# Score matmuls of an even and an odd head issued together, over two score banks, in one attention of a three-network kernel

## What is computed

```
scores = q[h] @ k[group].T / 8          # 256 x 512 for each head
o[h]   = softmax(scores) @ v[group]
cv     = depthwise_conv31(glu)          # 512 channels
y      = silu(layer_norm(cv) * g + b)
h      = h + gate * (concat(o, y) @ w_out)
```

## Time and profile before

| what | value |
|---|---|
| median of 3 runs | 2510.86 us |
| runs | 2505.34, 2510.86, 2511.07 us |
| profiled execution, its own time | 2511.8 us |
| its span in the profile | 2509.7 us |
| TensorE matmul busy | 2049.2 us (82% of the span) |
| VectorE busy | 586.2 us (23%) |
| ScalarE busy | 322.7 us (13%) |
| GpSimd busy | 122.8 us (5%) |
| mean DMA rate | 253 GB/s over the span |

### The profile page before, as it was taken

One profiled execution on the slowest core, in us unless ns is written; L12 is line 12 of the kernel. 1 busy time (PEld: TensorE's weight loads), 2 busy tenths in 40 slices (PEclk: granted clock), 3 DMA queues, 4 the chain that ended last, 5 costly groups with the idle time before them and its releaser, 6 DMA issues.

```text
span 2509.7 us, 30195 instructions
## 1 busy us (share of the span) xinstructions
PE 2049.2 (82%) x12607; PEld 1211.2 (48%) x12607; DVE 586.2 (23%) x1650; ACT 322.7 (13%) x784; POOL 122.8 (5%) x164
## 2 busy tenths in 40 slices
PE   7999999897555666798765656669899999979999
PEld 3444547564222222485322322234578744547874
DVE  1223335822000000223000000033524302332330
ACT  1023311221000000102000000011411101201110
POOL 0100003600000000000000000011000000000000
PEclk9999999589888778899978787879899999969999
DMA  9876763017999999953999999984044335303430
GB/s 356 325 262 228 277 209 137 31 59 305 425 426 426 426 427 426 323 191 120 424 425 427 426 426 425 426 308 154 31 134 157 145 105 181 101 18 125 160 118 17
DMA packets 190494, 634.46 MB, mean 253 GB/s; under 512 B 7393, under 2 KB 89457, under 8 KB 157640
## 3 DMA queue, kind: packets, MB, share of 16 engines
q1 hardware_dynamic: 186000, 623.84, 64.1%
q0 software_dynamic: 1472, 5.76, 0.6%
q10 hardware_dynamic: 2936, 3.66, 0.4%
HBM read 632.14 MB, written 1.09 MB: 252 GB/s over the span
## 4 chain that ended last, share of the span: by engine, by line
PE 62%; DMA 30%; DVE 5%; ACT 1%; issue 1%; POOL 1%; SPq 0%; POOLq 0%; DVEq 0%; ACTq 0%
DMA ring<-in_moe_w_down 30%; PE bank L573 18%; PE bank L588 16%; PE bank L2126 6%; PE bank L1788 4%; PE bank L669 2%; PE bank L901 2%; PE bank L632 2%; PE bank L859 2%; PE bank L660 2%; PE bank L497 1%; PE bank L1772 1%; PE bank L1805 1%; DVE arena L1339 1%; PE bank L1149 1%
## 5 line engine op out<-in xcount | busy, mean ns | idle before, releaser
L1772 PE MATMUL bank<-ring,arena 128*32 128x256 f32 x4096 | 316.3, 465 | 198.9 <-DMA ring<-in_moe_w_up 122.0
L588 PE MATMUL bank<-hT,ring 128*128 128x256 f32 x1920 | 423.2, 384 | 4.3 <-DVE arena L2167 3.0
L588 PEld LDWEIGHTS bank<-hT,ring 128*128 128x128 f32 x1920 | 369.8, 193 | 57.5 <-issue 6.1
L573 PE MATMUL bank<-ring,hT 128*128 128x512 f32 (+3 forms) x864 | 356.1, 571 | 7.9 <-DVE hT L523 3.5
L1772 PEld LDWEIGHTS bank<-ring,arena 128*32 128x32 f32 x4096 | 143.7, 128 | 357.5 <-DMA ring<-in_moe_w_up 158.8
L573 PEld LDWEIGHTS bank<-ring,hT 128*128 128x128 f32 x864 | 161.6, 192 | 191.7 <-issue 188.7
L1788 PE MATMUL bank<-ring,arena 128*32 128x256 f32 x2048 | 168.7, 488 | 83.0 <-DMA ring<-in_moe_w_down 73.7
L1788 PEld LDWEIGHTS bank<-ring,arena 128*32 128x32 f32 x2048 | 76.4, 134 | 162.2 <-DMA ring<-in_moe_w_down 80.6
L2126 PE MATMUL bank<-ring,arena 128*128 128x512 f32 x352 | 151.4, 592 | 0.0
L1628 DVE TENSOR_TENSOR arena<-arena,bank 128x256 f32<-128x256 f32 x32 | 13.5, 421 | 513.2 <-ACT arena L1688 513.2
L2126 PEld LDWEIGHTS bank<-ring,arena 128*128 128x128 f32 x352 | 66.9, 190 | 83.3 <-issue 83.2
(11 more groups left out here) (319 smaller groups left out, 1682.6 us busy)
## 6 DMA issues: line engine op xcount, KB each, us to landing
ring<-in_moe_w_gate SPq DMA_DIRECT2D x64, 2048.0 KB, 26.7
ring<-in_moe_w_up SPq DMA_DIRECT2D x64, 2048.0 KB, 26.1
ring<-in_moe_w_down SPq DMA_DIRECT2D x64, 2048.0 KB, 26.1
ring<-in_ada_w SPq DMA_DIRECT2D x24, 2048.0 KB, 13.0
ring<-in_w_up SPq DMA_DIRECT2D x44, 1024.0 KB, 7.5
ring<-in_w_in SPq DMA_DIRECT2D x11, 2048.0 KB, 13.3
ring<-in_w_down SPq DMA_DIRECT2D x10, 2048.0 KB, 7.9
ring<-in_w_out SPq DMA_DIRECT2D x6, 2048.0 KB, 7.9
```

What stands on the lines that cost most here:

```text
L573: ins = t_.matmul(bank[b][:, 0:n], lhsT(k)[:, P * t:P * t + P], w[:, k, c0:c0 + n], start=(k == 0), stop=(k == kt - 1))
L588: ins = t_.matmul(bank[b][:, 256 * (j % 2):256 * (j % 2) + 256], w[:, k, P * j:P * j + P], rhs[:, k, :], start=(k == 0), stop=(k == 7), sk ...
L1772: ins = t_.matmul(bank[4][32 * j:32 * j + 32, at:at + 256], xs_now[b][:, 4 * (c % 2) + k, :], w[:, k, 256 * j:256 * j + 256], start=(c % 2 ...
```

## The change

The even layer's attention goes through the same branch as the others: at an even step the scores of units i and i+1 are issued back to back, at an odd step none. `units2` is reordered so that the units of a pair are the two heads 2·h2 and 2·h2 + 1 with the same half of the queries. The score banks of this attention become TWO (4 and 2) on all three engines, so that the scores of unit i wait for the exponential of unit i-2. Nothing else is changed; the steps of the work beside the attention keep their numbers.

```diff
@@ attention_pe
             ahead = len(scores)
-            paired = tag != "b2"
...
             for i in range(len(units) + 3):
-                if i < len(units) and not paired:
-                    score_bank_free(i)
-                    score(i)
-                elif i < len(units) and i % 2 == 0:
+                if i < len(units) and i % 2 == 0:
                     score_bank_free(i)
                     score_bank_free(i + 1)
                     score(i)
                     score(i + 1)
@@ units2
-        for h in range(8):
-            g, lo = h // 4, HD * (h % 2)
-            for t in range(2):
-                units2.append(unit(pair(qxT, h, t), kxT[lo:lo + HD, g, :], [kv[:, k, P + HD * g:P + HD * g + HD] for k in range(4)],
-                                   512, qx[:, t, HD * h:HD * h + HD]))
+        for h2, t, m in itertools.product(range(4), range(2), range(2)):
+            h = 2 * h2 + m
+            g, lo = h // 4, HD * m
+            units2.append(unit(pair(qxT, h, t), kxT[lo:lo + HD, g, :], [kv[:, k, P + HD * g:P + HD * g + HD] for k in range(4)],
+                               512, qx[:, t, HD * h:HD * h + HD]))
@@ even_pe, even_act, even_dve
-            attention_pe("b2", units2, before=turned("kx", kx_items) + turned("qx", qx_items), also=layer_norm_sums)
+            attention_pe("b2", units2, before=turned("kx", kx_items) + turned("qx", qx_items), also=layer_norm_sums, scores=TWO)
-            attention_act("b2", units2, before=[(dve_s, "glu1")], also=squares)
+            attention_act("b2", units2, before=[(dve_s, "glu1")], also=squares, scores=TWO)
-            attention_dve("b2", units2, also=conv_and_norm)
+            attention_dve("b2", units2, also=conv_and_norm, scores=TWO)
```

## The result

The changed kernel takes 2516.2 us in the median of 14 runs, against 2511.59 us for the kernel before in its own 14. The ratio is 1.002, with a 95% interval of 1.0011 to 1.0029: 4.6 us slower by the medians, a difference that many runs resolve, though it lies inside the 0.3% that the prediction called no change. The forecast was 2517.3 us, from a working that gave +6.4.

A forecast was written before the change was run, and what follows sets the result against it. TensorE and VectorE were taken as tied in the even layer's attention. VectorE's stalls +5.3, steps 12 to 15 0 and clock +1.0 gave +6.3, say 6.4 us: median 2517.3 us, range 2507 to 2524.

The forecast's parts named there:

- What bounds the kernel: Even layer's attention: TensorE ends the chain, VectorE has no slack; at most some 1.5 us of TensorE's saving can count.
- The cost of a pair: Two 512-key score products of neighbouring heads overlap and cost what one does: 2.00 us low clock, 1.05 full.
- The wait and what is queued behind it: Even steps 4 to 10: late pairs delay P times V, stalling VectorE's output and the taps queued behind: +5.3 us.
- Steps 12 to 15 and the clock: End of the even layer's attention: later small sums offset by a saved score, 0; earlier clock fall, +1.0 us.
- After the stage: Behind the even layer's attention: nothing absorbs a shift; expert weights and the weight traffic move with the attention's end.
- A: Rival, slower: the clock does not come back at the layer-norm sums; +11 us, 2522 us; chance 0.18.
- B: Rival, faster: pairs keep the clock at 1.00 between them and VectorE never stalls; 7 us, 2504; chance 0.08.
- C: Rival, faster still: TensorE alone is the bound and its 14 us all count; 2497; chance 0.04.
- D: Rival, slower: the pair's products do not overlap, 4.00 us in place of 2.00; about +17, 2528; chance 0.04.

The follow-up runs named there:

- the three banks: The changed kernel with its pairs over three score banks in place of two: 2504.8 us, ratio 0.9976 to the kernel before.
- the few taps: The changed kernel with 58 of VectorE's 62 convolution instructions beside the attention left out: 2493.7 us; the kernel before with the same left out: 2508.6 us.
- the kernel that makes it so: The changed kernel with the old order of units, so both products of a pair lie in the same 64 partitions: 2527.0 us, ratio 1.007 to the kernel before.
- the outputs behind the taps: The changed kernel with VectorE's reciprocal and output of steps 0 to 10 put behind the step's convolution taps: 2515.8 us, ratio 1.0016 to the kernel before.

## Why the prediction was right

**What bounds the kernel.** Right. TensorE's 14.00 of 14.00 did not mean that 14 us could be had from it, since VectorE's 13.79 stood next to it; taking 15.7 us of busy time off TensorE gained nothing, and with the wait out of the way 1.1 us to the sums.

**The cost of a pair.** Right: by the chain 2.08 us at the low clock and 1.06 at the full one, for 2.00 and 1.05.

**The wait and what is queued behind it.** Right in place, sign and nearly in size. Forecast: stalls of 0.85, 0.85, 2.1 and 2.1 us ahead of VectorE's output at steps 4, 6, 8 and 10. Measured idle there: 0.31, 0.97, 0.17 + 1.85 and 0.16 + 2.00 (the smaller parts ahead of the row minimum). The layer-norm sums came 4.7 us late, for 5.3. The first stall is short because P times V took 1.16 us in that step, where it takes 1.81 at the low clock: the full clock came up within the step, which the working had at the low clock throughout. The second comes near its forecast by two shifts against each other: P times V took 1.32 us, and the six taps ahead of it 3.38 instead of 3.88.

**Steps 12 to 15 and the clock.** Forecast 0 + 1.0 us, measured -0.2. Several errors cancel here, which is luck. The clock fell in the gap ahead of unit 14's score (the pair took 2.08 us), and the small sums started 10.1 us behind step 12 instead of the 8.5 of the sum. But the full clock was back for them and for the transposes behind them, and it also came up sooner in the layer-norm sums, 2.64 us for 3.44. The term was sized as a loss; in this kernel the clock also came up where the working did not look for it.

Its size also rested on a misread row. The fall between 452 and 458 us was put down to some 3 us of near-idle time, a longer gap than the 2.08 us to come. TensorE's timeline of the kernel before has two gaps there, with 1.7 us of work between them, and the longer is no longer than the one to come:

```profile
455.01 0.66 PE L660 MATMUL bank<-const,p_buf 128*128 128x128 f32 x4 [2.08 <-ACT p_buf L701]
...
457.92 1.12 PE L660 MATMUL bank<-const,p_buf 128*128 128x128 f32 x4 [1.20 <-ACT p_buf L701]
```

The working's 1.5 us for small sums at the low clock was sized right: where that happened, they took 3.52 us for 1.90. And the clock of 0.50 from 470 to 484 us, which the prediction reads as agreement in sign, is none: there was no gap there that could have held it down.

**After the stage.** The weights that were issued at 540.74 go out at 545.88, and the chain of weight traffic begins at 624.83 instead of 619.41. Nothing absorbed the shift up to there, as forecast. But the last output came only 4.2 us later (the stage takes 4.6 us more and began 0.4 us earlier); 1.0 us more came from the output projection, which the working had at nothing. So the forecast had +5.3 to the sums and +1.0 behind them; the traces have +4.7, -0.2 and, behind the stage, +1.0. The medians say +4.6. The two pairs of traced executions differ by 2.7 and by 6.5 us in their spans, so the end of the program can't confirm the parts.

**The rivals.** A (the clock does not come back at the layer-norm sums) did not happen: 1.00 from 504 us, though TensorE had stood idle for 2.96 to 5.93 us ahead of every pair. B (the clock stays up between the pairs) did not happen either, but the clock came up within steps 4, 6 and 8 and was lost in the gap ahead of the next pair; it did stay up once VectorE's taps were gone, where it had a share in the 15 us. C falls with the three banks and the few taps: TensorE's time counts only when VectorE's does not. D was priced at +17 us; the kernel that makes it so took +16. That agrees in part by luck: to the sums it lost 11.8 us, and 3.3 us lie behind them, mostly in a clock that stayed low, for which D's working had nothing.

The loss belongs to no single edit: the order costs 0, two banks alone 2.1 us of the stage, pairs alone (over three banks) gain 3.8 to 6.7, both together lose 4.6. With two banks a pair waits for the exponential of the unit just ahead of it, and each such wait ends one block of taps later.

## What to carry to other kernels

Where two engines are both busy all the time, a cheaper instruction on one is worth only the slack of the other (1.1 us of 14 here); read both rows before summing. When work is issued in groups, count how far back the group's last member reaches: a group of two over two buffers waits for its direct neighbour, and one bank more took 8 us or more off the stage with the same pairs. Look at what is queued in order behind a late operand, and at TensorE's granted clock behind every gap that the edit makes.

## What the hardware showed that was not expected

- The granted clock followed more than how busy TensorE was: 15.00 of 15.00 us busy with single 64-partition scores was granted 0.50, 12.27 of 15.00 us with pairs of them and without the taps 1.00, and 5.00 of 5.00 us with pairs and the taps 0.50 again. What in the mix decides was not tried apart.
- A gap of 2.33 us ahead of the same pair came with three outcomes: in the kernel without the taps the clock stayed at 1.00 through it, in the changed kernel it fell and came back 3 us after the pair's start, and with the outputs behind the taps it fell and stayed low to the end of the stage, which cost 3 us. The last two were repeated in a second trace. What sets them apart stays open.
